# Head norms of the recurrence: roots moved from ScalarE's logarithm and exponential to GpSimd's power, and spread back by TensorE

## What is computed

```
kk = k * k_k
kk = kk / max(norm(kk, axis=-1), 1e-12)            # "kk": a sum of 64 squares, its root, a division
...                                                # the recurrence gives y
mean = mean(y, axis=-1)
var = mean(square(y - mean), axis=-1)
y = (y - mean) * rsqrt(var + 64e-5)                # "gn": a mean of 64 squares, its root, a division
y = y * gn_gain + gn_bias
```

## Time and profile before

| | |
|---|---|
| median of 3 runs | 1805.96 us (1805.27 to 1805.99) |
| profiled execution | 1805.27 us |
| its span, first to last instruction | 1803.5 us |
| TensorE busy | 1754.2 us (97%) |
| VectorE, ScalarE, GpSimd busy | 930.7, 832.8, 402.8 us |
| granted TensorE clock | 0.999 of full speed |

### The profile page before, as it was taken

One profiled execution on the slowest core, in us unless ns is written; L12 is line 12 of the kernel. 1 busy time (PEld: TensorE's weight loads), 2 busy tenths in 40 slices (PEclk: granted clock), 3 DMA queues, 4 the chain that ended last, 5 costly groups with the idle time before them and its releaser, 6 DMA issues.

```text
span 1803.5 us, 38565 instructions
## 1 busy us (share of the span) xinstructions
PE 1754.2 (97%) x16237; PEld 1402.0 (78%) x16237; DVE 930.7 (52%) x1976; ACT 832.8 (46%) x1838; POOL 402.8 (22%) x395
## 2 busy tenths in 40 slices
PE   9999999999999999999999999999999999999998
PEld 8997776788888688977777777776777876668887
DVE  5667766423533627116555555555445267765513
ACT  6346666434533525225535535535443356655421
POOL 5650000011111433213222122122223101002221
PEclk9999999999999999999999999999999999999999
DMA  5143320233243152342222122122223320006432
GB/s 199 47 155 107 85 56 1 88 100 112 88 120 114 54 181 97 86 125 92 65 62 78 54 73 77 54 73 72 67 64 121 99 68 13 1 1 210 157 135 94
DMA packets 146004, 159.89 MB, mean 89 GB/s; under 512 B 15092, under 2 KB 123960, under 8 KB 145832
## 3 DMA queue, kind: packets, MB, share of 16 engines
q1 hardware_dynamic: 145800, 157.37, 27.5%
q0 software_dynamic: 32, 0.07, 0.0%
HBM read 110.53 MB, written 52.62 MB: 90 GB/s over the span
## 4 chain that ended last, share of the span: by engine, by line
PE 87%; DVE 5%; ACT 4%; DMA 1%; issue 1%; POOL 1%; SPq 0%; DVEq 0%; POOLq 0%; ACTq 0%
PE ps L1003 8%; PE ps L701 7%; PE ps L703 7%; PE ps L702 7%; PE ps L1005 7%; PE ps L1004 7%; PE ps L1121 4%; PE ps L816 4%; PE ps L795 3%; PE ps L895 3%; PE ps L897 3%; PE ps L896 3%; PE ps L803 3%; PE ps L1309 3%; PE ps L1332 2%; PE ps L1319 2%
## 5 line engine op out<-in xcount | busy, mean ns | idle before, releaser
L2852 POOL TENSOR_TENSOR t<-t,t 128x512 fp32r<-128x512 f32 x183 | 240.6, 1327 | 877.9 <-ACT t L1436 831.0
L1003 PE MATMUL ps<-t,t 128*128 128x512 f32 (+2 forms) x720 | 291.4, 405 | 1.5 <-POOL t L2852 1.3
L701 PE MATMUL ps<-t,t 128*128 128x256 f32 (+2 forms) x872 | 282.6, 324 | 2.0 <-ACT t L1443 1.0
L702 PE MATMUL ps<-t,t 128*128 128x256 f32 (+2 forms) x872 | 276.7, 317 | 0.0
L703 PE MATMUL ps<-t,t 128*128 128x256 f32 (+2 forms) x872 | 276.7, 317 | 0.0
L1005 PE MATMUL ps<-t,t 128*128 128x512 f32 (+2 forms) x720 | 268.2, 372 | 0.0
L1004 PE MATMUL ps<-t,t 128*128 128x512 f32 (+2 forms) x720 | 267.7, 372 | 0.0
L701 PEld LDWEIGHTS ps<-t,t 128*128 128x128 f32 x872 | 165.9, 190 | 18.7 <-issue 7.5
L702 PEld LDWEIGHTS ps<-t,t 128*128 128x128 f32 x872 | 166.0, 190 | 10.3 <-issue 0.4
L703 PEld LDWEIGHTS ps<-t,t 128*128 128x128 f32 x872 | 165.9, 190 | 10.4
L1003 PEld LDWEIGHTS ps<-t,t 128*128 128x128 f32 x720 | 135.7, 188 | 37.2 <-issue 14.1
(11 more groups left out here) (270 smaller groups left out, 3175.3 us busy)
## 6 DMA issues: line engine op xcount, KB each, us to landing
t<-in_w_in SPq DMA_DIRECT2D x53, 512.0 KB, 5.9
zgate_spill<-t SPq DMA_DIRECT2D x20, 512.0 KB, 2.9
tile_bias<-t SPq DMA_DIRECT2D x16, 576.0 KB
t<-tile_bias SPq DMA_DIRECT2D x8, 1152.0 KB, 5.8
t<-zgate_spill SPq DMA_DIRECT2D x16, 512.0 KB, 4.1
feat_spill<-t SPq DMA_DIRECT2D x13, 512.0 KB, 3.2
tile_bias<-band_bias SPq DMA_DIRECT2D x48, 128.0 KB
t<-values_and_gates SPq DMA_DIRECT2D x96, 64.0 KB
```

The lines of the kernel that those rows point to most:

```text
L701: e.matmul(dst, lh, rh, start=k == 0, stop=False)
L702: e.matmul(dst, lh, rl, start=False, stop=False)
L1003: e.matmul(dst, lh, rh, start=k == 0, stop=False)
L2852: e.tensor_tensor(WLO[wslot(b)][:, o], WST[:, o], WHI[wslot(b)][:, o].bitcast(F), ALU.subtract).then_inc(w_lo.sem, w_lo.up((b, p)))
```

## The change

The sums of squares are now made with the squares as the stationary operand. For each half of the 256 tokens one matmul multiplies them (128 channels x 128 tokens) by a constant of two columns (ones for the first head, ones for the second). The result has tokens on the partitions: 128x2 for each half, 128x4 in all, instead of 128x256. VectorE turns this into a floored sum or a mean plus epsilon in a small buffer (`head_mean`), GpSimd raises it to the power -0.5 and copies it out over 64 channels into a new buffer HX of 128x256 (`spread`), and TensorE turns HX back to channels on partitions by two products with the identity (`head_spread`). VectorE multiplies by that, straight from PSUM. The two activations per norm and the early loads of ScalarE's table are gone. For "kk" the sum stays at step 2, `head_mean` and `spread` are at step 2 of their engines, `head_spread` at step 4. For "gn" the spread comes two steps after the sum, and the norm has one step of NORM_US more, so that a unit takes 27 steps. On ScalarE the Exp of step 4 (line 1765) now also waits for `head_spread`. On VectorE the difference `tm` now stands ahead of the scaling of `kk`.

```diff
@@ pe_program, unit
-                def head_sums(sq, ready, key, blocks):
-                    ps = mine(key, (norm_a, (u, key, "log")))
+                def head_sums(sq, ready, key):
+                    ps = mine(key, (norm2_v, (u, key, "mean")))
                     w.wait_ge(*ready)
-                    m = e.matmul(ps[:, 0:TU], cst(blocks, 128), sq[:, :], start=True, stop=True)
-                    m.then_inc(prep_mm.sem, prep_mm.up((u, key)))
+                    for m in range(MP):
+                        i = e.matmul(ps[:, 2 * m:2 * m + 2], sq[:, tile128(m)], cst(C_ONE2, 2), start=True, stop=True)
+                    i.then_inc(prep_mm.sem, prep_mm.up((u, key)))
+
+                def head_spread(key, emptied):
+                    w.wait_ge(*prep_p[u, key, "spread"])
+                    ps = mine((key, "spread"), emptied)
+                    for m in range(MP):
+                        l = S.HX[:, 2 * m:2 * m + 2, :].rearrange("p h c -> p (h c)")
+                        i = e.matmul(ps[:, tile128(m)], l, ident, start=True, stop=True)
+                    i.then_inc(prep_mm.sem, prep_mm.up((u, key, "spread")))
...
-                head_sums(E2, prep_a[u, "kk2"], "kk", C_BLK)
-                for _ in range(3):
-                    yield STAGE_US
+                head_sums(E2, prep_a[u, "kk2"], "kk")
+                yield STAGE_US
+                yield STAGE_US
+                head_spread("kk", (prep_v, (u, "kn")))
+                yield STAGE_US
...
-                head_sums(E1, norm2_v[u, "yc2"], "gn", C_BLKM)
+                head_sums(E1, norm2_v[u, "yc2"], "gn")
                 yield STAGE_US
+                yield NORM_US
+                head_spread("gn", (norm2_v, (u, "scaled")))
                 yield NORM_US
                 yield NORM_US
@@ act_program, unit
-                head_roots("kk", E2, dict(scale=65536.0), dict(bias=cst(C_EPS, 1)))
                 yield STAGE_US
                 yield STAGE_US
-                logs_and_exponentials()
                 w.wait_ge(*prep_v[u, "tm"])
+                w.wait_ge(*prep_mm[u, "kk", "spread"])
                 e.activation(E2[:, :], TM[:, :], ACT.Exp, scale=-CD).then_inc(prep_a.sem, prep_a.up((u, "e2")))
...
                 yield NORM_US
-                head_roots("gn", E1, dict(bias=cst(C_EPS + 1, 1)), {})
                 yield STAGE_US
-                yield NORM_US
+                for _ in range(2):
+                    yield NORM_US
                 yield NORM_US
@@ dve_program, unit
+                def head_mean(key, c0, mul, add, floor):
+                    w.wait_ge(*prep_mm[u, key])
+                    if floor is None:
+                        i = e.tensor_scalar(STAT[:, c0:c0 + CU_], psum((u, key))[:, 0:CU_], mul, add, ALU.mult, ALU.add)
+                    else:
+                        i = e.tensor_scalar(STAT[:, c0:c0 + CU_], psum((u, key))[:, 0:CU_], floor, None, ALU.max)
+                    i.then_inc(norm2_v.sem, norm2_v.up((u, key, "mean")))
...
-                w.wait_ge(*norm_a[u, "kk", "root"])
-                e.scalar_tensor_tensor(out=KK[:, :], in0=E2[:, :], scalar=1e12, in1=KK[:, :], op0=ALU.min, op1=ALU.mult).then_inc(*did("kn"))
                 w.wait_ge(*prep_v[u, "v1"])
                 e.tensor_tensor(TM[:, :], CU[:, :], SG[:, :], ALU.subtract).then_inc(*did("tm"))
+                w.wait_ge(*prep_mm[u, "kk", "spread"])
+                w.wait_ge(*prep_a[u, "kk2"])
+                e.tensor_tensor(KK[:, :], KK[:, :], psum((u, ("kk", "spread")))[:, 0:TU], ALU.mult).then_inc(*did("kn"))
...
                 yield NORM_US
+                head_mean("gn", 288 + 64 * n, 1.0 / 64, 64e-5, None)
                 yield STAGE_US
-                w.wait_ge(*norm_a[u, "gn", "root"])
-                w.wait_ge(*norm2_v[u, "yc"])
-                e.tensor_tensor(YT[:, :], YT[:, :], E1[:, :], ALU.mult).then_inc(*normal("scaled"))
+                yield NORM_US
+                w.wait_ge(*prep_mm[u, "gn", "spread"])
+                w.wait_ge(*norm2_v[u, "yc2"])
+                e.tensor_tensor(YT[:, :], YT[:, :], psum((u, ("gn", "spread")))[:, 0:TU], ALU.mult).then_inc(*normal("scaled"))
@@ pool_program, unit
+                def spread(key, c0, spread_before):
+                    w.wait_ge(*norm2_v[u, key, "mean"])
+                    power(STAT[:, c0 + 8:c0 + 8 + CU_], STAT[:, c0:c0 + CU_], CU_, (u, key))
+                    if spread_before:
+                        w.wait_ge(*prep_mm[spread_before])
+                    w.wait_ge(*power_p[u, key])
+                    e.tensor_copy(S.HX[:, :, :], bc(STAT[:, c0 + 8:c0 + 8 + CU_], 2, 64)).then_inc(prep_p.sem, prep_p.up((u, key, "spread")))
```

More of the change, by code:

```diff
@@ L23 @@
 C_ID, C_CAUS, C_BLK, C_BLKM = 0, 128, 256, 384
-C_MD, C_MS, C_MI, C_MDT, C_MOT, C_I64, C_INV, C_EPS = 512, 576, 640, 704, 768, 832, 896, 912
+C_MD, C_MS, C_MI, C_MDT, C_MOT, C_I64, C_INV, C_ONE2 = 512, 576, 640, 704, 768, 832, 896, 912
 C_END = 914
@@ L59, in constants @@
     c[:, C_INV:C_INV + 16] = (np.float32(10000.0) ** (-np.arange(0, 32, 2, dtype=np.float32) / np.float32(32)))[None]
-    c[:, C_EPS] = np.log(256.0)
-    c[:, C_EPS + 1] = 64e-5
+    c[:64, C_ONE2] = 1.0
+    c[64:, C_ONE2 + 1] = 1.0
     inv = np.float32(10000.0) ** (-np.arange(16, dtype=np.float32) * np.float32(2.0 / 32))
@@ L119 @@
     tensor_copy = tensor_reduce = reciprocal = memset = tensor_tensor_scan = dma_start = then_inc = nothing
-    wait_ge = preload_act_table_set = nothing
+    wait_ge = nothing
 class Waits:
@@ L269, in __init__ @@
                 self.BHN, self.KHN, self.VNN = (self.buf([128, CU_ // 2, 128]) for _ in range(3))
-                self.DG = self.buf([128, CU_, 64])
+                self.DG, self.HX = (self.buf([128, CU_, 64]) for _ in range(2))
                 self.BD, self.IF, self.FT, self.FN = (self.buf([128, CU_, 64]) for _ in range(4))
@@ L1712, in dense @@
                         e.activation(o, i, ACT.Copy).then_inc(dense_out.sem, dense_out.up(key))
-            table = set()
-            def logs_and_exponentials():
-                if not table:
-                    e.preload_act_table_set("natural_log_exp_and_others")
-                    table.add("natural_log_exp_and_others")
             def unit(il, u):
@@ L1728, in unit @@
                 before = u - 2
-                def head_roots(key, dst, log, root):
-                    logs_and_exponentials()
-                    w.wait_ge(*prep_mm[u, key])
-                    e.activation(dst[:, :], psum((u, key))[:, 0:TU], ACT.Ln, **log).then_inc(norm_a.sem, norm_a.up((u, key, "log")))
-                    w.wait_ge(*norm_a[u, key, "log"])
-                    e.activation(dst[:, :], dst[:, :], ACT.Exp, scale=-0.5, **root).then_inc(norm_a.sem, norm_a.up((u, key, "root")))
                 if u < 2:
@@ L1747, in unit @@
                 w.wait_ge(*vec_v["vec"])
-                table.clear()
                 for name, dst, bias in (("decay", SG, "w0"), ("rate", AI, "a0")):
@@ L2473, in unit @@
                 yield STAGE_US
+                head_mean("kk", 256 + 64 * n, None, None, 1e-24)
                 yield STAGE_US
@@ L3010, in unit @@
                 yield STAGE_US
+                spread("kk", 256 + 64 * n, (before, "gn", "spread") if before >= 0 else None)
                 yield STAGE_US
@@ L3060, in unit @@
                 yield NORM_US
+                spread("gn", 288 + 64 * n, (u, "kk", "spread"))
                 yield STAGE_US
-                yield NORM_US
-                yield NORM_US
+                for _ in range(3):
+                    yield NORM_US
             def late():
```

## The result

| | before | after |
|---|---|---|
| device time, median (range) of 4 runs, us | 1805.68 (1805.27 to 1805.99) | 1817.34 (1816.79 to 1818.21) |
| profiled execution / its span, us | 1805.27 / 1803.5 | 1818.21 / 1816.4 |

The ratio is 1.0065, with a 95% interval of 1.0048 to 1.0083: slower by 11.7 us. The forecast was slower by 17.9 with a range of 1809 to 1838; sign and range hold, the size is 6 us too large. The whole difference arises there.

The account below looks back on a forecast made before the run. The prediction took TensorE's instruction stream, busy 97% of the span, as the bound. Its terms, 13.9 + 0 + 5 + 3 - 4 = 17.9 us on 1805.3, gave 1823 us, with an 8-in-10 range of 1809 to 1838.

Parts of the forecast that it names:

- The spreads: On TensorE, 32 new spreads of four passes 0.11 us apart, paid in full: 13.9 us, upper bound 15.
- The sums: On TensorE, four two-column passes take 0.44 us against 0.43 now: costed at nothing, bounds -7 and +4 us.
- The wait for GpSimd: TensorE's spreads wait for GpSimd's power and copy, 8 of 24 behind a low part: 5 us, bounds 0 and 32.
- Centring: At an even unit's end, TensorE's centring waits for VectorE, busy with "gn": 8 waits, 3 us, bounds 0 and 7.
- What is given back: ScalarE's relief shortens TensorE's waits of sums for the square: credit 4 us, bounds 0 and 22.3.
- The added step: One step more per unit moves 13 dense groups forward from the remainder behind the units: zero.
- A: Rival: faster; VectorE and ScalarE on time everywhere, TensorE's waits vanish: -8.4, 1797 us; chance 4%.
- B: Rival: no change; relief of 10 to 17 us just pays the passes: 1802 to 1809 us; chance 6%.
- C: Rival: GpSimd late at all 24 spreads by one low part: 46 us more, 1851 us; chance 9%.
- D: Rival: GpSimd's added work slows VectorE operations where TensorE waits next: 11 us more, 1834 us; chance 8%.
- E: Rival: weight loads of the 128 new TensorE passes stand in the open: +14 us, 1837 us; chance 3%.
- F: The forecast itself: passes paid in full, waits nearly cancel: 1811 to 1832 us; chance 70%.

Follow-up runs that it names:

- run 8: Kernel before without ScalarE's roots and their early table loads, and with four idle 128-column TensorE passes for each of the 32 norms: 1811.02 us, +4.8.
- run 3: Kernel before without ScalarE's Ln, Exp of the root and early table loads; VectorE multiplies by the sum straight from PSUM: 1797.18 us, -8.7.
- run 7: Kernel after with GpSimd's copy made twice at each of the 32 factors: 1818.09 us, +11.9 against the kernel before.
- run 11: Kernel after with the spread of "kk" and VectorE's product with it one step later: 1819.07 us, +13.5 against the kernel before.
- run 6: Kernel after without the added step, so 26 steps a unit; VectorE gates the output in the step that scales it: 1817.76 us, +11.5 against the kernel before.
- run 10: Kernel before with the square of "kk" made by VectorE right behind kk, not by ScalarE: 1805.63 us, ratio 1.0.
- run 9: Kernel before with VectorE's difference ahead of the kk factor; ScalarE's Exp of step 4 also waits for the scaling: 1806.88 us, ratio 1.0007.
- run 1: Kernel before with four idle 128-column TensorE passes added for each of the 32 norms, roots kept: 1814.9 us, +9.0.
- run 4: Kernel before with only the one step more in each unit, between the sum of gn and its scaling: 1810.31 us, +4.4.
- run 12: Kernel before with difference ahead of factor (Exp waiting for the scaling), square of kk on VectorE, and VectorE's bonus product one step earlier: 1802.58 us, -2.9.
- run 5: Kernel before with the new way for "kk" alone; "gn" keeps its ScalarE activations and units their 26 steps: 1814.26 us, +8.0.
- run 2: Kernel after with each spread's products made twice: 1827.55 us, +21.7 against the kernel before.

## Why the prediction was right, and where its size was off

**The spreads, 13.9 us.** Right. 128 passes 0.111 us apart are 14.2 us of TensorE, and run 8 against run 3 measured 13.5 in the time, 12.2 in the stage. The rule that the prediction quotes from the Trainium skill, TensorE: Matmul & The Clock Gate, section "The mechanism", is contradicted by the new passes as well, as far as it stands alone: they use all 128 rows, each has its own load, and 78 of the 96 spacings inside the spreads are 0.108 to 0.113 us. The other 18, each the first of its spread, are 0.19 to 0.22 us; those spreads stand behind a sum, a 64-row product or a wait.

**The sums, 0 us.** Nearly right: 0.46 against 0.43 us between dense passes, 0.55 behind a 64-row product, some 1 us in all. The bound of "tiny passes at half that spacing" was not met: the two passes of one product do start 0.03 us apart, but the loads between products make up for it.

**The wait for GpSimd, 5 us.** The size is right (4.1 in the list). So is the cause, but not the count: it was to be 8 of 24 spreads, 0.6 us each, behind a low part of the weights that mostly waits for ScalarE first. It is three, all of "kk", at 820, 1041 and 1254 us, waiting 1.0 to 1.7 us, and each of the three has such a low part right ahead of its power. (The slack that it compared with, 0.1 to 1.2 us, reaches 3.9 - 2.4 = 1.5 us by its own figures; that changes little.) The longest (VectorE's mean, then GpSimd, then the spread):
```profile
1035.66 0.16 DVE L2448 TENSOR_SCALAR t<-ps 128x4 f32<-128x4 f32 x1 [1.21 <-PE ps L1034]
1037.53 1.30 POOL L2857 TENSOR_TENSOR t<-t,t 128x512 fp32r<-128x512 f32 x1 [2.88 <-ACT t L1449]
1038.79 1.19 POOL L2863 TENSOR_TENSOR t<-t,t 128x4 f32<-128x4 f32 x1
1040.11 0.40 POOL L3009 COPY t<-t 128x256 f32<-128x256 f32 x1
1040.56 0.71 PE L1042 MATMUL ps<-t,t 128*128 128x128 f32 x4 [1.65 <-POOL t L3009]
```
The mean was there at 1035.82, but the queue stood until 1037.53 before a low part for which ScalarE was late. Run 7 shows that all other spreads have over 0.47 us to spare. And it is no price of its own: where run 11 took it away, more than the whole came back at the bonus product.

**Centring, 3 us.** 1.8 in the list, three waits and not eight. Run 6 brought it to 0.8 without any gain in time.

**What is given back, 4 us.** The way is the one that the prediction gave, but the term is too small. In the kernel before, all four late squares stand behind an Exp of step 4 that waited for VectorE's difference, which stood behind the scaling. The longest, engine by engine:
```profile
1027.78 1.51 DVE L2482 SCALAR_TENSOR_TENSOR t<-t,t 128x256 f32<-128x256 f32 x1
1029.66 0.42 ACT L1765 ACTIVATE t<-t 128x256 f32<-128x256 f32 x1 [2.73 <-DVE t L2484]
1032.11 0.41 ACT L1753 ACTIVATE t<-t 128x256 f32<-128x256 f32 x1
1032.67 0.67 PE L1033 MATMUL ps<-t,t 128*128 128x256 f32 x2 [2.03 <-ACT t L1753]
```
Alone, the roots were worth 8.7 us (run 3), 5.7 in the stage of the profiled execution. If the distance between two starts of TensorE is put down to the later of the two, 5.4 of these 5.7 us are had at the sums, and nothing elsewhere above 0.5. Run 10 does not speak against it. There the sums give 5.6 us by the same count, but the bonus product takes 3.2 of them back and the dense products, with the spell at half clock, 1.4. Run 3 has a shorter way through VectorE than run 10: no added square, no root to wait for and a quicker product with "kk" (0.42 us against 0.58), and its bonus product waits 9.6 us as before. Which part of the relief in the changed kernel comes from the new order of difference and scaling is open, since run 9 held the Exp back.

In the changed kernel the list shows more relief than 4 us: without the two new rows, of spreads and centring, it holds 16.0 of the former 22.3 us. 4.3 of these 6.3 are the sums' wait for the square; the rest are small rows, of which the prediction credited none, less the 1.2 by which the bonus wait grew. With what was measured for each term, 14.2 + 1 + 4.1 + 1.8 - 6.3 = 14.8 us, against 17.9 forecast, 13.3 in the stage of the profiled executions and 11.7 between the medians.

**The sum.** In the order of the runs: roots out, -8.7 (run 3); passes in as well, +4.8 (run 8); from there to the kernel after, at +11.7, another 6.9. The prediction had -4 + 13.9 = 9.9 where run 8 has 4.8, and 5 + 3 + 0 = 8 for the 6.9. Of its error of 6.2 us, 5.1 lie in the pair and 1.1 in the rest. Both terms of the pair can be found in the runs, but in different kernels: the full price of the passes where the roots are gone already (13.5, beside -8.7), the small credit where the passes are there already (-4.2, beside 9.0). Taken in either order they give 4.8; taken as the prediction did, they leave out the 4.5 us of slack on which both draw. The rows show where it lies: the sums' wait for the square, 4.7 us before, is 0.5 without the roots, 1.4 with the passes, and not in the list with both, so each alone takes most of the same wait. The intervals of these runs are 4 to 5 us wide, and by the lengths of the stage in the profiled executions (+9.5 in run 1, -5.7 in run 3, +6.5 in run 8) the passes cost 9.5 with the roots and 12.2 without, so the shared part is 2.7; it is some 3 to 5 us.

**The rest, +6.9.** The stage of the kernel after is 6.9 us longer than that of run 8 too (673.2 against 666.4). Summed over the distances between TensorE's starts in these two traces, put down as above, the spreads take 4.7 us more than the idle passes, centring 2.3, the bonus 0.9, the sums 0.8 and the dense products, the spell at half clock included, 0.4; the products of 64 rows and the chain take 2.6 less. That names 6.5 of the 6.9. That GpSimd's way lies behind the whole is not shown piece by piece: taking single waits out (runs 6 and 11) did not bring it back.

**The added step, zero.** Right inside the change, by run 6, but the reason given does not carry. The prediction looked only at the dense groups that the step moves, and in the kernel before, where it moves the same, the step costs 4.4 us (run 4): the sums meet ScalarE late for 4.3 us more there, and two spells at half clock come with it. The changed kernel has next to nothing of that wait to lengthen; that this is the whole of the difference is not shown.

**The clock, no term.** Nearly right: a spell at half clock stands in the stage after, where before had none. TensorE at its place:
```profile
987.95 0.70 PE L1083 MATMUL ps<-t,t 128*128 128x256 f32 x2 [2.26 <-DVE t L2506]
...
990.58 0.63 PE L1003 MATMUL ps<-t,t 128*128 128x512 f32 x1
991.01 0.63 PE L1004 MATMUL ps<-t,t 128*128 128x512 f32 x1
...
992.11 0.40 PE L1004 MATMUL ps<-t,t 128*128 128x512 f32 x1
992.34 0.39 PE L1005 MATMUL ps<-t,t 128*128 128x512 f32 x1
```
Behind the wait of 2.26 us dense passes start 0.43 us apart, then 0.23 again from 992.11: 1.2 GHz for 3.4 us, which costs 1.7. The windows (span, busy by engine, granted clock, DMA share, GB/s) agree:
```profile
985.00:990.00 5.00, 2.74 (x20) 2.31 (x13) 3.89 (x9) 1.66 (x6) 1.13 (x1) 0.85 0.25 101
990.00:995.00 5.00, 5.00 (x68) 3.76 (x68) 1.24 (x4) 0.71 (x2) 1.59 (x2) 0.81 0.32 108
995.00:1000.00 5.00, 5.00 (x164) 4.06 (x166) 2.35 (x7) 2.30 (x6) 1.89 (x3) 1.00 0.02 5
```
The spell does not decide the sign of the result: run 6 has none in the stage and takes as long.

**The rivals.** A and B (relief of 10 us or more) are out: 8.7 alone, 4.2 beside the passes. C (GpSimd late at all 24) is out by run 7, though its mechanism is that of the three waits. D (VectorE slowed by GpSimd) is out at its size: VectorE is busy 328.2 us from 790 to 1450 us, less than the 342.6 before, though some of its groups are longer (its product for the bonus 647 ns on average, from 595), which may be part of the bonus wait's 1.2. E (loads in the open) is out by the spacing. F came true, in its lower third, with its passes not quite paid in full.

## What to carry to other kernels

Price a pair of edits in one order: what an added piece costs, and what a removed one gives, both depend on the slack the other leaves, and two prices from two kernels don't add. A row in the bound engine's list of waits says where it meets a late chain, not what is gained by curing that row. In the seven runs that add no pass and take out no root (4, 6, 7, 9 to 12) the sum of all rows moved with the time to within 1 us, from -3.4 us in the list and -2.9 in the time (run 12) to +4.0 and +4.4 (run 4), each against the kernel that it was made from, while in run 10 a row of 4.7 us went away with none of it in the time. It is no law: in run 3 the list fell by 3.8 us and the time by 8.7. So before crediting a row, ask which engine's way leads to the next wait (here VectorE's, through the factor to the bonus product), and whether the edit shortens that way. Work that is added in the bound engine's own stream can be priced from the trace of before, by the spacing of starts of the same form.

## What the runs showed of the hardware

**VectorE's product with "kk".** Its group before (count, busy us, mean ns, idle before), beside that of the kernel after, shown with run 11:
```profile
L2482 DVE SCALAR_TENSOR_TENSOR t<-t,t 128x256 f32<-128x256 f32 x16 | 10.1, 629 | 1.5 <-ACT t L1735 1.5
```
With both inputs in SBUF it took 629 ns on average and 418 in the median; with one input in PSUM it took 416 on average in run 3, 418 in run 8, and 414 in the kernel after, where GpSimd has 47 us more to do. The difference just ahead of it, two SBUF inputs, still averages 616. Before, the five products that took 735 ns or more all began while a GpSimd operation ran, and each ended 0.28 to 0.29 us behind that operation's end; the others took 416 to 421. In run 3 six of the 16 ran beside a GpSimd operation, and none took over 425. The Trainium skill's page SBUF — State Buffer, section "Who interferes with whom", says that a VectorE instruction with at most one SBUF input, outside the modes that use both ports, doesn't contend with GpSimd, and these rows agree.

**Half clock after a wait.** In the stage, the kernels of the twelve runs and the two of the case had eight TensorE waits of 2.2 to 2.6 us between them; six were followed by 3.4 us at half clock that had begun within 1 us of the wait's end (runs 4, 5, 7, 10, 12 and the kernel after), two were not (2.26 in run 2, 2.23 in run 11). Waits of 2.03 to 2.12 (before, runs 7 and 9) were not; yet one of 1.87 in run 7, one of two of 1.86 in run 4 and one of 1.41 in run 5 were, 1.1 to 1.8 us behind their ends. The same wait of 1.41 in the kernel after was not. The length of the wait alone does not decide it.
